# Moving each expert tile's down projection between two parts of the next tile's gate and up projection

## The reference, cut to what matters

```
combine = one_hot(top-2 experts of the top group) * weights     # 16 experts
a   = einsum('bsd,edf->bsef', h, w_gate)      # d = 1024, f = 256
u   = einsum('bsd,edf->bsef', h, w_up)
hid = silu(a) * u * combine
x   = x + einsum('bsef,efd->bsd', hid, w_down)
```

## Time and profile before

| | us |
|---|---|
| median of 3 runs | 507.0 (506.62 to 509.67) |
| the profiled execution's own time | 506.83 |
| its span, first to last instruction | 505.1 |
| TensorE busy in the span | 461.6 (91%) |
| mean granted TensorE clock | 0.968 of full speed |
| DMA over the span | 102.12 MB, mean 202 GB/s |

### The profile page before, as it was taken

The page is one execution under the profiler, slowest core; times in us unless marked ns, Lnnn a source line. Parts: engine busy times, 40 slices in busy tenths (PEclk is TensorE's granted clock), DMA queues, the critical chain, the costliest instruction groups (busy, mean ns, idle before and its releaser), DMA issues.

```text
span 505.1 us, 7636 instructions
## 1 busy us (share of the span) xinstructions
PE 461.6 (91%) x2816; PEld 226.3 (45%) x2816; DVE 220.1 (44%) x688; ACT 145.8 (29%) x332; POOL 153.1 (30%) x163
## 2 busy tenths in 40 slices
PE   5999999989999999999999989519999999999982
PEld 3544545444555565555456556523333333333320
DVE  2144755525765545355566757607322222222210
ACT  1322504225455566444342533300000010110000
POOL 1151288877399910000000212200063111111121
PEclk9999999989999999999999999659999999999998
DMA  8999950006100000193000449973999999999731
GB/s 319 387 405 370 403 201 1 1 0 224 46 2 0 1 1 1 31 414 139 0 3 1 131 157 384 380 299 102 351 297 380 385 375 387 388 374 404 258 57 26
DMA packets 28745, 102.12 MB, mean 202 GB/s; under 512 B 3744, under 2 KB 5280, under 8 KB 28320
## 3 DMA queue, kind: packets, MB, share of 16 engines
q1 hardware_dynamic: 22080, 86.12, 44.0%
q0 software_dynamic: 4176, 8.42, 7.0%
q10 hardware_dynamic: 2448, 7.04, 3.8%
HBM read 79.48 MB, written 28.91 MB: 215 GB/s over the span
## 4 chain that ended last, share of the span: by engine, by line
PE 69%; DMA 8%; DVE 7%; POOL 7%; issue 4%; SPq 2%; ACT 1%; POOLq 0%; DVEq 0%
PE bank L1620 14%; PE bank L1298 14%; PE bank L1465 10%; PE bank L1641 6%; PE bank L1282 6%; DMA arena<-in_w_gu 6%; PE bank L1387 5%; PE bank L1370 5%; POOL small L477 3%; PE bank L1604 2%; SPq L393 2%; PE bank L1491 2%; PE bank L1411 2%; PE bank L1475 1%; DMA slot_rows<-arena,small 1%
## 5 line engine op out<-in xcount | busy, mean ns | idle before, releaser
L1298 PE MATMUL bank<-arena 128*128 128x512 f32 (+1 forms) x256 | 111.3, 585 | 5.6 <-DMA arena<-in_w_in_lat 5.6
L1620 PE MATMUL bank<-arena 128*32 128x512 f32 x832 | 92.6, 596 | 0.9 <-DMA arena<-in_w_gu 0.9
L1298 PEld LDWEIGHTS bank<-arena 128*128 128x128 f32 x256 | 48.3, 195 | 53.9 <-issue 53.9
L606 POOL DMA_INDIRECT out<-arena x13 | 20.2, 1551 | 138.7 <-DVE arena L1232 100.2
L1282 PEld LDWEIGHTS bank<-arena 128*128 128x128 f32 (+1 forms) x348 | 41.5, 139 | 37.5 <-issue 31.9
L1465 PE MATMUL bank<-arena 128*128 128x512 f32 x112 | 54.1, 605 | 0.5 <-issue 0.5
L1282 PE MATMUL bank<-arena 128*128 128x128 f32 (+1 forms) x348 | 49.8, 275 | 4.5 <-DVE arena L954 2.8
L1620 PEld LDWEIGHTS bank<-arena 128*32 128x32 f32 x832 | 26.1, 110 | 57.9 <-issue 56.8
L1641 PE MATMUL bank<-arena 128*32 128x512 f32 x416 | 47.1, 592 | 0.5 <-DVE arena L1225 0.5
L963 DVE COPY arena<-bank 128x512 f32<-128x512 f32 (+2 forms) x64 | 35.8, 581 | 20.9 <-PE bank L1282 20.9
L837 ACT ACTIVATE arena<-bank 128x256 f32<-128x256 f32 x13 | 5.0, 384 | 131.5 <-PE bank L1620 131.5
(11 more groups left out here) (163 smaller groups left out, 506.3 us busy)
## 6 DMA issues: line engine op xcount, KB each, us to landing
arena<-in_w_gu SPq DMA_DIRECT2D x17, 2048.0 KB, 20.2
arena<-in_w_dn SPq DMA_DIRECT2D x17, 1024.0 KB, 20.5
slot_rows<-arena SPq DMA_DIRECT2D x1, 11308.0 KB, 46.4
arena<-slot_rows ACTq DMA_DIRECT2D x13, 514.0 KB, 6.8
arena<-in_w_out SPq DMA_DIRECT2D x2, 2048.0 KB, 8.3
arena<-in_x_turned SPq DMA_DIRECT2D x4, 512.0 KB, 7.8
arena<-in_x SPq DMA_DIRECT2D x4, 512.0 KB, 13.2
arena<-in_w_in_k SPq DMA_DIRECT2D x1, 2048.0 KB, 14.7
```

Of the source, the lines that this page charges most:

```text
L1298: last = nc.tensor.matmul(product_bank(i)[:, 0:width], hT[:, t, k, :], w[:, k, :], start=(k == 0), stop=(k == KD - 1))
L1620: last = nc.tensor.matmul(GU[g % 2][BLK * b:BLK * (b + 1), :], xT[g % 2][:, k, BLK * b:BLK * (b + 1)], w_gu[n % RING][:, k, :], start=(k = ...
```

## The change

In blocks 1 to 11 TensorE now does what it did in block 12 alone: two steps of gate_up(g), then down(g - 1), then the other six steps. ScalarE evicts the left half of tile g - 1 ahead of silu(g), and VectorE the right half ahead of the hidden product of tile g. The order of the loads on SyncE and their waits stand as they were, and nothing is added or taken out. Block 0 has no down projection and block 12 had this order before.

```
--- before.py
+++ after.py
@@ -845,15 +845,13 @@
             for g in range(LAST + 1):
-                if g == LAST:
+                if g > 0:
                     left_y(g - 1)
                 silu(g)
                 if g + 4 <= LAST:
                     if g + 4 == LAST:
                         act.wait_ge(s_over, 16 * TOP * T)
                     load_x(g + 4)
-                if 0 < g < LAST:
-                    left_y(g - 1)
             left_y(LAST)
@@ -1250,11 +1248,9 @@
             for g in range(LAST + 1):
-                if g == LAST:
+                if g > 0:
                     right_y(g - 1)
                 hidden(g)
-                if 0 < g < LAST:
-                    right_y(g - 1)
                 if g + 2 <= LAST:
                     x_read(g + 2)
                     tile_tags(g + 2)
@@ -1647,10 +1643,10 @@
             x_turns(0)
             x_turns(1)
             for g in range(LAST + 1):
-                gate_up(g, range(2 if g == LAST else KD))
+                gate_up(g, range(2 if g > 0 else KD))
                 if g > 0:
                     down(g - 1)
-                if g == LAST:
+                if g > 0:
                     gate_up(g, range(2, KD))
                 if g + 2 <= LAST:
                     x_turns(g + 2)
```

## The result

The changed kernel takes 517.04 us (median of 4 runs, 515.47 to 518.09) against 506.97 before, a ratio of 1.0183 with a 95% interval of 1.0164 to 1.0203. Measured again beside 13 runs of the kernel before it took 515.92 against 508.09, 1.0136 (1.0088 to 1.0184). So it is slower by 1.4 to 1.8%, more than forecast: the first time lies above the range, the second 0.4 us above its upper end.

A forecast was written before the change was run, and what follows sets the result against it. TensorE and the DMA engines were both taken as near their limits. The last late weight load lands at 476.3, plus 9.95 us starts block 12 at 486.3 instead of 479.58: +6.7 on 506.83 gives 513.5 us, range 510 to 515.5.

The forecast's parts named there:

- The hidden turns: TensorE, blocks 1 to 11: they lose the down projection as cover, 0.17 us in each of ten blocks, 0.91 in block 11.
- The cover of the next down projection: Two steps of gate_up cover hidden_read, 0.2 us early: nothing charged, up to 0.2 us a block as upper bound.
- dn 14 as the load that sets block 12: Last late load, for down(10) in block 11: lands at 476.3 in place of 473.3, so block 12 starts at 486.3.
- gu 6 issued 3.4 us later: SyncE, start of the expert stage: this gate and up load goes at 361.5 in place of 358.05.
- Every us that these idle stretches grow is a us by which all later weights land later: DMA engines idle in two early stretches awaiting SyncE's issues; the first grows 3.4 us, making weights 2.6 to 3.4 late.
- D = 3.0: Assumed lateness of the weight stream in us, between 2.6 and 4.8; these ends give 513.1 and 515.3 us.
- the add of tile 9: GpSimd's output add, issued some 2 to 5 us earlier, overtakes queued weights: up to 1.4 us, in the upper end only.
- The wait for dn 10: Block 8: down(7) asks at 435.6, when this load landed before, so with the stream late it waits 3 us.
- Rival (d): Clock falls at a wait for down weights: 4.6 us at half rate, 2.3 us of work lost, 515.8 us; chance 0.05.
- (a): Weights not later, since a full queue holds most issues; dn 14 still awaited: +3.7, 510.5 us; chance 0.22.
- (b): Not slower: earlier adds and scatters let weights land in time; only the hidden turns count, +1.7, 508.5 us; chance 0.12.
- (c): Faster: earlier down projections let weights run ahead, hidden turns cost nothing, 0.94 us go: 505.9 us; chance 0.03.

The follow-up runs named there:

- the pair without reloads: Kernel before and changed kernel, each with weight loads 5 to 16 left out: 506.44 and 509.68 us, one run each; blocks 1 to 12 take 127.6 and 130.2 us.
- order_alone: Changed kernel with only TensorE's new order, the evictions left where they were before: 517.35 us, ratio 1.0208 to the kernel before.
- late_gu: Kernel before, with SyncE also waiting for down(g - 1) before it issues the gate and up loads: 509.10 us, ratio 1.0015.
- blocks_from_3: Changed kernel with the new order in blocks 3 to 11 only, blocks 1 and 2 in the old order: 515.88 us, ratio 1.0158.

## Why the prediction was wrong

**Right.** What bounds the kernel was right, and so was the sign. The hidden turns: 0.17 us in ten blocks and 0.91 in block 11 were forecast, 2.6 in all; the pair without reloads shows 130.2 - 127.6 = 2.6. The cover of the next down projection holds: no down projection of blocks 1 to 12 waits for hidden_read, and order_alone shows that it has less than 0.2 us to spare (0.75 us more on VectorE became 0.62 on TensorE). Right too were dn 14 as the load that sets block 12, over 2 us of wait for it in block 11, and gu 6 issued 3.4 us later (measured 3.5).

**Wrong in its reason.** The step that failed is the sentence "Every us that these idle stretches grow is a us by which all later weights land later", from which D = 3.0 was worked out. late_gu has the same late issues and brings gu 14 0.4 and dn 14 0.4 us late, with its queue some 1.5 us behind in bytes. blocks_from_3 has no late issue there, has its other loads on time, and keeps 7.8 of the 8.7 us. That dn 14 came 3.3 us late and D was 3.0 is a coincidence. Some 2.2 us of it go when the adds go back. The prediction had priced the add of tile 9 at up to 1.4 us and kept it out of D, as an upper end only. The last 1 us is the lateness of the whole stream, whose cause is not settled. The wait for dn 10, 3 us by this D, was 0.4 in one profile and 1.0 in the other. In its place stood a wait that the prediction does not name, 1.30 and 0.95 us in block 10 for dn 13.

**Wrong in size.** The clock. Rival (d) said that it might fall in the wait for dn 14 and cost 2.3 us, with a chance of 0.05, on the ground that the waits "lie in full streams". It fell there in both profiles of the changed kernel, and costs 1.3 to 1.7 us. This term, put at nothing in the sum, is most of what separates the 8.7 us of the stage from the forecast's 6.7: dn 14 landed 0.3 us later than forecast, and of the 11.4 us from the start of down(10) to block 12, where the sum has 9.95, 1.3 are the clock's.

**Chance.** The forecast of 513.5 missed the 517.04 by 3.5 us. Of these the stage has 2.0 and the front the rest: 1.6 us of the 10.1 lie in front of the stage, where the profile of the kernel before began earliest of fourteen. The sum was made on that one profiled execution. In the second measurement the difference of the medians is 7.8 us, below the 8.7 of the stage.

**The rivals.** (a) and (b) asked whether the weights come later. The reason of (a), that the issue's time does not matter over most of the stage, came near (0.4 us at dn 14 in late_gu); its result did not, for the adds. (c) did not happen.

## What to carry to other kernels

Before an operation is moved up past its weights' landing, put the landing time of each of its loads beside the time at which it will now ask, and add to that list whatever else the move sends out earlier on other queues: here the loads' own issue, 3.5 us later, made dn 14 0.4 us late, and the output adds, 2 to 4 us earlier for tiles 2 to 9, another 2.2. A queue that is behind in bytes does not make each of its loads late by as much; only an experiment that delays the issue alone tells. And where a new wait of some us opens in a stream of matmuls, count the slower clock behind it as part of its price, and try whether the order of the loads can be turned to the new order of use, which here gave back 4.7 of 8.7 us.

## What the runs showed of the hardware

- Of a queue of weights that was 0.6 MB behind 40 us into the stage and 0.55 MB at 115 us, with the DMA share at 1.0 between, the loads landed 3.5 us late (gu 7), 2.6 (gu 12), 0.5 (gu 13) and 0.4 (dn 14).
- An indirect add of at most 0.5 MB issued 115 to 116 us after block 1 landed 9.1 us later, and dn 14, issued 20 us before that add, 0.4 to 0.5 us behind it. With the add issued at 118.4 to 120.0 us, dn 14 landed at 122.4 to 123.5 us in place of 124.5 to 125.7.
- One wait of 3.05 to 3.07 us for a DMA, after 125 us of matmuls without a gap longer than 1.5 us, was enough for the clock to go to 1.2 GHz; the down projection behind it took 4.95 to 5.34 us in place of 3.6. The same arrival with 2.8 us of matmuls in the wait left it at 2.4 GHz.
- The start of block 1 moved by 3.3 us between profiles of programs whose work is the same up to there.
